# Softmax division folded into the transposition: exponents turned by a product with a diagonal of reciprocal row sums

## What is computed

```
def blocked_attention(q, k, v):
    ...
    def one_block(qi):
        s = jnp.einsum('bqkgd,btkd->bkgqt', qi, k).astype(jnp.float32) * scale
        p = jax.nn.softmax(s, axis=-1).astype(v.dtype)
        return jnp.einsum('bkgqt,btkd->bqkgd', p, v)

def neighbourhood_attention(q, k, v, ctx_k, ctx_v, rpb):
    ...
        s_win = s_win.reshape(b, hh, GRID_W, kr * kc) * scale + bias.astype(jnp.float32)
        s_ctx = jnp.einsum('bqhd,bphd->bhqp', qr, ctx_k).astype(jnp.float32) * scale
        p = jax.nn.softmax(jnp.concatenate([s_win, s_ctx], axis=-1), axis=-1).astype(v.dtype)
    ...
        return (jnp.einsum('bhqrj,brqjhd->bqhd', p_win, vw)
                + jnp.einsum('bhqp,bphd->bqhd', p_ctx, ctx_v))
```

## Time and profile before

| | us |
|---|---|
| median of 3 runs | 1665.0 (1661.41 to 1667.53) |
| the profiled execution, its own time | 1667.2 |
| its span | 1665.4 |
| stage of attention, layer 0 | about 256 to 301 |
| stage of attention, layer 1 | about 1010 to 1075 |
| TensorE busy, over the span | 1516.3 |
| VectorE busy | 445.5 |
| ScalarE busy | 304.9 |

### The profile page before, as it was taken

How to read it: one execution, slowest core, us unless ns; L and a number is a source line. 1 busy time by engine, 2 the same in 40 slices (tenths; PEclk the granted TensorE clock), 3 DMA queues, 4 the chain that set the end, 5 groups by cost and what they waited for, 6 DMA issues and landing times.

```text
span 1665.4 us, 21436 instructions
## 1 busy us (share of the span) xinstructions
PE 1516.3 (91%) x8387; PEld 723.5 (43%) x8387; DVE 445.5 (27%) x1055; ACT 304.9 (18%) x649; POOL 145.8 (9%) x200
## 2 busy tenths in 40 slices
PE   5999887979999999999958998896999999999991
PEld 4455784444433333333314555544333333333330
DVE  0012586433111111111123025633311111111113
ACT  3100225211111111111121005511111111111112
POOL 1002111100000000000005000100000000000001
PEclk9999887978999999999988999997999999999995
DMA  9999962245999999999969522103999999999982
GB/s 349 331 335 179 384 223 104 81 177 220 428 427 428 428 428 428 428 427 427 428 252 309 184 101 77 53 28 144 408 428 428 427 428 427 429 428 428 427 345 117
DMA packets 82919, 521.56 MB, mean 313 GB/s; under 512 B 10130, under 2 KB 11610, under 8 KB 56240
## 3 DMA queue, kind: packets, MB, share of 16 engines
q1 hardware_dynamic: 69536, 485.58, 71.4%
q0 software_dynamic: 13328, 35.22, 6.9%
HBM read 511.01 MB, written 20.22 MB: 319 GB/s over the span
## 4 chain that ended last, share of the span: by engine, by line
PE 88%; DVE 7%; ACT 2%; DMA 1%; issue 1%; POOL 0%; POOLq 0%; DVEq 0%; ACTq 0%
PE psum L896 26%; PE psum L909 14%; PE psum L877 10%; PE psum L543 6%; PE psum L842 5%; PE psum L565 5%; PE psum L562 3%; PE psum L902 3%; PE psum L467 2%; PE psum L889 2%; PE psum L883 2%; PE psum L764 1%; PE psum L509 1%; PE psum L751 1%; PE psum L789 1%
## 5 line engine op out<-in xcount | busy, mean ns | idle before, releaser
L896 PE MATMUL psum<-ring,area_t 128*64 128x512 f32 x1024 | 449.9, 592 | 1.8 <-issue 0.9
L897 PE MATMUL psum<-ring,area_t 128*64 128x512 f32 x1024 | 450.0, 593 | 0.0
L896 PEld LDWEIGHTS psum<-ring,area_t 128*64 128x64 f32 x1024 | 140.1, 137 | 291.8 <-issue 291.8
L909 PE MATMUL psum<-ring,area_t 128*64 128x512 f32 x1024 | 235.6, 602 | 2.3 <-DVE area_t L1864 2.3
L1835 DVE COPY area_q<-psum 64x512 f32<-64x512 f32 x64 | 44.4, 694 | 567.2 <-PE psum L897 567.2
L877 PE MATMUL psum<-area_h,area_t 128*64 128x512 f32 x768 | 180.8, 607 | 3.0 <-DVE area_t L1849 3.0
L2048 POOL DMA_INDIRECT pair_rows<-area_q,idx x64 | 62.4, 975 | 932.3 <-ACT area_q L1267 932.3
L897 PEld LDWEIGHTS psum<-ring,area_t 128*64 128x64 f32 x1024 | 140.2, 137 | 0.0
L909 PEld LDWEIGHTS psum<-ring,area_t 128*64 128x64 f32 x1024 | 69.1, 137 | 123.2 <-issue 123.2
L1257 ACT ACTIVATE area_q<-psum 64x512 f32<-64x512 f32 x64 | 37.8, 590 | 403.3 <-PE psum L897 403.3
L877 PEld LDWEIGHTS psum<-area_h,area_t 128*64 128x64 f32 x768 | 56.6, 140 | 113.7 <-issue 110.5
(11 more groups left out here) (265 smaller groups left out, 1396.7 us busy)
## 6 DMA issues: line engine op xcount, KB each, us to landing
ring<-in_moe_w SPq DMA_DIRECT2D x192, 2048.0 KB, 14.8
ring<-in_ada_w SPq DMA_DIRECT2D x24, 2048.0 KB, 20.0
ring<-in_na_w_in SPq DMA_DIRECT2D x6, 2048.0 KB, 17.2
ring<-in_ab_w_in SPq DMA_DIRECT2D x5, 2048.0 KB, 18.7
area_m<-mod_ready POOLq DMA_DIRECT2D x6, 1024.0 KB, 9.3
area_q<-pair_rows POOLq DMA_DIRECT2D x6, 1024.0 KB, 7.3
ring<-in_ab_w_out SPq DMA_DIRECT2D x2, 2048.0 KB, 20.8
area_g<-mod_ready POOLq DMA_DIRECT2D x4, 1024.0 KB, 8.8
```

The source lines that it names most:

```text
L896: pe.matmul(banks[2 + u][0:64, :], lhsT, w1[:, k, :], start=(k == 0), stop=(k == KT - 1))
L897: mm = pe.matmul(banks[2 + u][64:128, :], lhsT, w3[:, k, :], start=(k == 0), stop=(k == KT - 1))
L909: mm = pe.matmul(banks[6 + u][64 * j:64 * j + 64, :], hidT[u][:, k, :], w2[:, k, 512 * j:512 * j + 512], start=(k == 0), stop=(k == 3))
```

## The change

VectorE no longer multiplies the exponents. After the reciprocal of the row sums it writes, for each of the unit's two heads, a 128x128 diagonal of these reciprocals: the identity times the reciprocals, one `tensor_tensor` of 128x256 for a unit of either size. TensorE then turns each 128x128 tile of undivided exponents with a `matmul` whose moving operand is that diagonal, in place of `transpose` with the identity. The result in PSUM is the transposed and divided tile. The diagonals (`shares`) stand in columns 1536 to 2047 of `area_g`, one half for even and one for odd units. The semaphores, their counts and the order of the instructions on each engine stay.

```diff
@@ -200,6 +200,7 @@
         prob = area_g[:, 0:1536].rearrange("p (b h n) -> p b h n", b=2, h=2)
+        shares = area_g[:, 1536:2048].rearrange("p (b h n) -> p b h n", b=2, h=2)
@@ -761,7 +762,8 @@
                     for s in range((k1 - k0) // P):
-                        mm = pe.transpose(banks[4 + hh][:, s * P:s * P + P], prob[:, U % 2, hh, s * P:s * P + P], ident)
+                        mm = pe.matmul(banks[4 + hh][:, s * P:s * P + P], prob[:, U % 2, hh, s * P:s * P + P],
+                                       shares[:, U % 2, hh, :], start=True, stop=True)
                 mm.then_inc(S["probT_done"], 1)
@@ -1685,14 +1687,11 @@
                 def normalise(i):
                     U = U0[l] + i
-                    k0, k1 = keys_of(unit(i)[1])
                     col = 2 * (U % 4)
                     v.wait_ge(S["prob_ready"], U + 1)
                     do(v.reciprocal(rlsum[:, col:col + 2], lsum[:, col:col + 2]))
-                    for hh in range(2):
-                        p = prob[:, U % 2, hh, 0:k1 - k0]
-                        ins = v.tensor_scalar(p, p, rlsum[:, col + hh:col + hh + 1], None, ALU.mult)
-                    ins.then_inc(S["prob_scaled"], 1)
+                    v.tensor_tensor(shares[:, U % 2, :, :], lead(ident, 2), last(rlsum[:, col:col + 2], P), ALU.mult)\
+                        .then_inc(S["prob_scaled"], 1)
```

## The result

The changed kernel takes 1674.86 us (median of 5 runs, 1672.13 to 1677.71) against 1665.0 before (5 runs, 1661.41 to 1667.53). The ratio is 1.0061, with a 95% interval of 1.0046 to 1.0077: 10 us slower, between 8 and 13. The forecast was 1678.0, with 1671 to 1685 as its range.

What follows compares the result with a forecast made beforehand. The prediction took the chain of waits inside the two attention stages as the bound. Longer TensorE steps of 18.3 us, less 4.4 on VectorE and a 0.9 correction, gave +13 us: a median of 1678, range 1671 to 1685.

Steps and rivals of the forecast that it cites:

- The passes of a product: Turning step on TensorE: a float32 product is two passes 0.11 us apart, adding 0.70 us per large unit.
- The other count, four transpositions per product: Rival at the turning step: one product costs four transpositions' time, large steps grow 1.98 us, total 1706; chance 0.02.
- VectorE's tile: Division on VectorE: one 128x256 multiplication of 0.43 us replaces two, gaining 0.33 us per large unit.
- What is on the chain: Layer 1's period per head pair: two large turning steps and one large division count, 7.12 us becoming 8.2.
- the term of the cold steps: Both attention stages: four of 23 large turning steps run at about half clock, each growing 1.25 us.
- the clock rival: Both attention stages: full clock returns, up to 8 us back plus 2.2 of surcharge, total 1668; chance 0.12.
- all three stretches: Half-clock attention at 268 to 272, 288 to 296 and 1014 to 1022 us, costing 2.6 + 6.6 + 6.9.
- Nothing elsewhere: Outside the two attention stages: everything stays as it was, only later, and the delay reaches the program's end undiminished.
- The +3.4 of the forecast: Layer 0's attention: its share of the forecast, from seven of eight large turning steps less five large divisions, +3.4 us.

Runs made afterwards that it cites:

- VectorE's half alone: Against the kernel before: VectorE writes the diagonal in place of its multiplications, TensorE still transposes with the identity, the division is left out; ratio 0.9973, -4.5 us.
- the pair of runs on the first units: Against the kernel before: the change only in layer 1's first three units, ratio 0.998; its mirror, only in layer 1 from the fourth unit on, ratio 1.0048.
- products with the identity: Against the kernel before: exponents still divided by VectorE, but turned by a float32 product with the identity in place of a transposition; ratio 1.0077, +12.8 us.

## Why the prediction was right, and where it was off

**The passes of a product: right.** Two records for a product, 0.11 us apart; a large step of 1.60 us where 1.61 was worked out from L617. The growth per large step was 0.72 us on the chain in place of the +0.70 that was taken. The other count, four transpositions per product, is refuted by the same records and the 1.60 us. At the half clock the step was sized low: the large unit at 289.63 us of the changed kernel took 2.93 us, 1.39 more than the 1.54 of a transposed one and not the 1.25 that was taken; the bound of +1.4 was right.

**VectorE's tile: right.** 0.425 us, 0.33 gained per large division. VectorE's half alone gave -4.5 us (-2.0 to -7.0) where the sum had -4.4.

**What is on the chain: right for layer 1.** Two large steps and one division per period: 8.2 forecast, 8.25 measured. The wait that covers the small step shrank to the 0.4 us that was said.

**The size, 13 against 10: the term of the cold steps, and with it the clock rival.** Cold steps are those at half clock. The prediction priced two of layer 1's large steps so (2 x 1.25 us) and gave the return of the clock 0.12, as a case that decides only if more than half of all three stretches returns. In layer 1 the clock came back whole. The account of that stage: 8 x 1.13 us of longer periods = 9.0, less 2.6 for the clock (from the pair of runs on the first units) = 6.4, and 71.0 - 64.6 = 6.4 was measured. The same account fits both halves: 8 x 1.46 - 2.6 = 9.1 for products with the identity (73.7 - 64.6 = 9.1), and 8 x 0.32 = 2.6 less with the clock as before for the diagonal (64.6 - 62.1 = 2.5). The prediction had +9.6 us for layer 1 (16 large steps, eight divisions of large units, one of a small one). The rival was thus half right: at 1014 to 1022 us it happened, and in layer 0 the clock fell again at about 289.5 us. The prediction's argument against it, that TensorE's wait for VectorE remains, held for the fall in layer 0 for which it was made, and does not carry over to layer 1: with products by the identity the waits for VectorE are those of before (0.36 and 1.11 us) and the clock stayed full. That the forecast's range held in spite of this term is partly its width: 1674.86 lies inside 1671 to 1685, 3 us below the middle.

**Layer 0: not settled.** The profiled stages are 44.8 us before and 46.8 after. But the kernels that leave layer 0 alone show 42.6 to 45.7, and with it changed alone the stage took 45.7 while the whole kernel measured +6.3 us (4.2 to 8.5). By the profiles its part is 0.9 or 2.0, by the run times 4 or more. The +3.4 of the forecast lies between the two and is neither confirmed nor refuted. Stretches at half clock in this stage sum to 10 to 20 us without order between transposed and multiplied kernels. TensorE here waits for the other mixer's work on VectorE, as at 284 to 288 us.

**Nothing elsewhere: right between the stages, not settled around them.** From the end of layer 0's attention to the start of layer 1's the two profiles differ by 0.3 us: the delay passed through the stream of weights undiminished. Of the 10.0 us between the two spans, 2.0 and 6.4 lie in the two stages. Another 2.4 arose ahead of the first, where the code is the same, and behind the second the changed kernel was 1.2 us shorter. So the profiles put the change at 8.4 to 8.7 us, at the low end of the 8 to 13 of the runs, and nothing here ties the rest of the +10.0 to the change.

## What to carry to other kernels

Count float32 work on TensorE in records, not in instructions of the program: a transposition by `transpose` is one pass, the same shape by `matmul` is two, and a fused scale costs that second pass for each tile. Before work is moved from one engine to another, look which of its pieces the chain of waits charges: here two enlarged steps per period against one shortened. A scale along rows that commutes with the next product can be applied behind it: here that was the cheapest of the three places, where the result is smallest and is copied anyway. Three units turned by products at the start of layer 1 were worth more in clock than they cost (-3.3 us, between -5.8 and -0.8); the same was not seen in layer 0.

## What was not expected

At the start of layer 1, with the division ahead of the turning, the clock went with the kind of pass. With twice the transpositions it fell, with as many product passes it did not, and what differed up to the fall was one small unit. Without the wait for the division it held with transpositions too. The 7 us at half clock cost 2.6 us, not the 3.4 that halving them would give, since in part of the stretch TensorE waits (it is busy for 2.72 of the 4 us from 1014 to 1018).

Code ahead of the attention is the same in all these kernels, yet layer 0's attention began anywhere between 253 and 259 us in their profiles. This spread of 5 us in the first sixth of the program is nearly the spread between the runs of the kernel before (1661 to 1668), and half of the effect that was studied. It is why stages, not totals, carry the argument here.
